# Up projections of two squared-ReLU layers as seven block products each (Strassen's scheme)

## The reference

```python
D_FF_2 = 4 * D_MODEL            # 4096
def sqrelu_mlp(h, w1, w2):
    a = jnp.square(jax.nn.relu(h @ w1))
    return a @ w2
...
h = h + sqrelu_mlp(rmsnorm_2(h, mlp_norm[i]), mlp_w1[i], mlp_w2[i])
```

## Time and profile before

| what | value |
| --- | --- |
| three executions | 2059.59, 2059.64 and 2062.62 us, median 2059.64 |
| profiled execution: span from first to last instruction | 2057.4 us |
| its instructions | 31378 |
| PE, weight loads (PEld), DVE, ACT, POOL busy | 1962.2, 1617.8, 1056.4, 742.9, 1060.0 us |
| DMA engines, mean busy share of the hardware queue | 31.8%, 80 GB/s read |

### The profile page before, as it was taken

One profiled execution on the slowest core, in us unless ns is written; L12 is line 12 of the kernel. 1 busy time (PEld: TensorE's weight loads), 2 busy tenths in 40 slices (PEclk: granted clock), 3 DMA queues, 4 the chain that ended last, 5 costly groups with the idle time before them and its releaser, 6 DMA issues.

```text
span 2057.4 us, 31378 instructions
## 1 busy us (share of the span) xinstructions
PE 1962.2 (95%) x10733; PEld 1617.8 (79%) x10733; DVE 1056.4 (51%) x1640; ACT 742.9 (36%) x1263; POOL 1060.0 (52%) x591
## 2 busy tenths in 40 slices
PE   8999989899999999889999999999998899999997
PEld 5679967778878787667778888887877788888886
DVE  6797846836687776796342313232137724222132
ACT  4335444533222224354432222233227642222223
POOL 5566747356747545662554444455445264444442
PEclk9999999999999999999999999999999999999999
DMA  4344013153333332101323333334346333333332
GB/s 138 78 112 117 23 42 98 31 113 92 95 89 102 92 92 78 36 2 33 100 84 102 92 102 92 92 94 108 94 109 156 84 100 101 92 102 92 97 94 86
DMA packets 345028, 181.87 MB, mean 88 GB/s; under 512 B 28527, under 2 KB 336103, under 8 KB 344935
## 3 DMA queue, kind: packets, MB, share of 16 engines
q1 hardware_dynamic: 343872, 179.91, 31.8%
q10 hardware_dynamic: 1062, 0.75, 0.1%
HBM read 162.73 MB, written 2.10 MB: 80 GB/s over the span
## 4 chain that ended last, share of the span: by engine, by line
PE 57%; issue 13%; POOL 9%; DVE 7%; POOLq 6%; ACT 3%; DVEq 2%; DMA 1%; SPq 1%; ACTq 0%
PE ACC L1625 16%; PE ACC L1631 16%; PE ACC L1626 16%; POOL WL L1254 7%; POOLq L1268 2%; POOLq L1479 1%; POOLq L1467 1%; PE ST L2097 1%; PE ACC L1797 1%; POOL GC L1478 1%; ACT WH L627 1%; POOL GT L1466 1%; SPq L586 1%; DVE DS L2281 1%; PE O L1754 0%
## 5 line engine op out<-in xcount | busy, mean ns | idle before, releaser
L1254 POOL TENSOR_TENSOR WL<-RAW,WH 128x1024 fp32r<-128x1024 f32 (+1 forms) x292 | 691.0, 2369 | 730.9 <-ACT WH L627 674.7
L1625 PE MATMUL ACC<-PH,WH 128*128 128x512 f32 x1248 | 493.6, 395 | 8.1 <-DVE PL L2206 2.8
L1626 PE MATMUL ACC<-PL,WH 128*128 128x512 f32 x1248 | 488.4, 391 | 0.0
L627 ACT ACTIVATE WH<-RAW 128x1024 fp32r<-128x1024 f32 (+1 forms) x292 | 301.0, 1032 | 450.3 <-PE ACC L1631 413.5
L1625 PE MATMUL ACC<-QH,WH 128*128 128x512 f32 (+1 forms) x1136 | 429.4, 382 | 12.7 <-ACT WH L627 6.9
L1626 PE MATMUL ACC<-QL,WH 128*128 128x512 f32 (+1 forms) x1136 | 425.7, 379 | 0.0
L1631 PE MATMUL ACC<-PH,WL 128*128 128x512 f32 x1248 | 312.8, 393 | 0.0
L1625 PEld LDWEIGHTS ACC<-PH,WH 128*128 128x128 f32 x1248 | 235.7, 189 | 66.3 <-DVE PL L2206 4.4
L1631 PE MATMUL ACC<-QH,WL 128*128 128x512 f32 (+1 forms) x1136 | 270.5, 379 | 6.5 <-POOL WL L1254 3.7
L1631 PEld LDWEIGHTS ACC<-PH,WL 128*128 128x128 f32 x1248 | 234.5, 188 | 52.7 <-issue 3.3
L1626 PEld LDWEIGHTS ACC<-PL,WH 128*128 128x128 f32 x1248 | 235.7, 189 | 48.8 <-issue 1.0
(11 more groups left out here) (448 smaller groups left out, 2548.3 us busy)
## 6 DMA issues: line engine op xcount, KB each, us to landing
RAW<-in_mlp_w_dram SPq DMA_DIRECT2D x128, 512.0 KB, 4.0
RAW<-in_w_gate_dram SPq DMA_DIRECT2D x22, 512.0 KB, 3.8
RAW<-in_w_up_dram SPq DMA_DIRECT2D x22, 512.0 KB, 3.8
RAW<-in_w_in_dram SPq DMA_DIRECT2D x16, 512.0 KB, 3.9
RAW<-in_w_down_dram SPq DMA_DIRECT2D x16, 512.0 KB, 4.1
RAW<-in_ssm_w_glu_dram SPq DMA_DIRECT2D x16, 512.0 KB, 3.8
RAW<-in_w_kvf_dram SPq DMA_DIRECT2D x16, 512.0 KB, 4.0
RAW<-in_w_out_dram SPq DMA_DIRECT2D x16, 256.0 KB, 2.8
```

The costliest lines, as they stand in the source:

```text
L627: act.activation(WH[:, s, 0:kc], RAW[:, s, 0:kc], ACT.Copy).then_inc(w_hi, 1)
L1254: pool.tensor_tensor(WL[:, s, 0:kc], RAW[:, s, 0:kc], WH[:, s, 0:kc], ALU.subtract).then_inc(w_lo, 1)
L1625: pe.matmul(ACC[s][:, 0:n], WH[:, s, k, :], xh[:, k, :], start=(k == 0), stop=False)
L1626: pe.matmul(ACC[s][:, 0:n], WH[:, s, k, :], xl[:, k, :], start=False, stop=False)
```

## The change

In each of the two layers, the eight up units of a group become two quads q. A quad is 512 hidden channels by 512 tokens by 1024 contracted channels, seen as a 2 x 2 block matrix product in Strassen's scheme (Winograd's form): the rows split into the even and the odd chunks of 128 channels, the columns into two pairs of 128, the tokens into two halves. Seven products (FAST = 7) take the place of eight blocks; a product is 24 matmuls of 256 columns.

Weights: SP loads the four blocks A11, A12, A21, A22 (two buffers of the last) of a quad, and DVE makes four sums of them: S1 = A21 + A22, S3 = A11 - A21, S2 = S1 - A11, and later S2 = A12 - S2. ACT rounds and POOL makes the remainder of each of the seven factors A11, S1, S2, A12, S3, S2, A22, into a ring of three slots. Operand: per pair of chunks DVE makes seven halves or differences of halves (TS, 128 x 256 each) where one scaled tile stood, ACT rounds them to FBH (two, then five of them) and DVE makes FBL. Results: banks FA and FE (two each) and FB; ACT copies three intermediate banks (PC1, PC5, PC6), DVE adds them to banks to make the blocks of HB, applies relu and RS, ACT squares and rounds, DVE makes the low part. The sums of the next quad, or of the next group during its last down units, are placed between these on DVE. The memsets of POOL move behind layer 0. The eight matmuls that keep PE busy at the start of either layer are gone.

```diff
+FAST = 7
-_MLP = [[(f"{_n}{_l}{_g}", 8) for _g in range(GROUPS) for _n in ("up", "dn")] for _l in range(2)]
+_MLP = [[(f"{_n}{_l}{_g}", {"up": 2 * FAST, "dn": 8}[_n]) for _g in range(GROUPS) for _n in ("up", "dn")] for _l in range(2)]
...
+RING = (2, 1, 0)
+OPERAND = (1, 0, 2, 5, 3, 6, 4)
...
+        def factor(n, j):
+            return (A11, S1, S2, A12, S3, S2, A22[n % 2])[j][:]
...
+            def round_factor(l, g, q, j):
+                n, u = quad_index(l, g, q), quad_unit(l, g, q) + j
+                if j in (0, 3, 6):
+                    k = {0: 0, 3: 1, 6: 3 + n % 2}[j]
+                    act.wait_ge(blk_in[k], BLK + 16 * ((n if j < 6 else n // 2) + 1))
+                else:
+                    act.wait_ge(s_made, 4 * n + {1: 1, 2: 3, 4: 2, 5: 4}[j])
+                act.wait_ge(unit_done, u - 1 if q == 0 and j == 1 else u - 2)
+                act.activation(high_weights(q, j), factor(n, j), ACT.Copy).then_inc(w_hi, 1)
...
+            def operand_high(l, i, b):
+                cols = slice(2, 7) if b else slice(0, 2)
+                act.wait_ge(ts_ready, TSR + KC * l + 2 * i + b + 1)
+                of = TS[:, 3:8, :] if b else TS[:, 0:2, :]
+                act.activation(FBH[l][:, bass.ds(i, 1), cols, :].rearrange("p o j t -> p (o j) t"), of, ACT.Copy).then_inc(op_hi, 1)
+                square(norm, 2 * i + b, X, b)
...
# ACT, in mlp(l), one group
+                    round_factor(l, g, 0, 1)
+                    for q in range(2):
+                        round_factor(l, g, q, 2)
+                        if q:
+                            block_squared(g, 0, 2)
+                        copied(l, g, q, 1)
+                        round_factor(l, g, q, 3)
+                        if q:
+                            block_high(g, 0, 2)
+                            block_squared(g, 0, 3)
+                        copied(l, g, q, 2)
...
+                        round_factor(l, g, q, 4)
+                        if q:
+                            block_high(g, 0, 3)
+                        copied(l, g, q, 3)
+                        round_factor(l, g, q, 5)
+                        round_factor(l, g, q, 6)
+                        block_squared(g, q, 0)
+                        if q == 0:
+                            round_factor(l, g, 1, 0)
...
+                        block_high(g, q, 0)
+                        block_squared(g, q, 1)
+                        if q == 0:
+                            round_factor(l, g, 1, 1)
+                        block_high(g, q, 1)
...
# POOL
+            def remainder_factor(l, g, q, j):
+                n, u = quad_index(l, g, q), quad_unit(l, g, q) + j
+                pool.wait_ge(w_hi, u + 1)
+                pool.tensor_tensor(low_weights(q, j), factor(n, j), high_weights(q, j), ALU.subtract).then_inc(w_lo, 1)
...
# PE
+            def product(l, g, q, j):
+                n, u = quad_index(l, g, q), quad_unit(l, g, q) + j
+                bank_ = (FA[n % 2], FE[n % 2], FA[n % 2], FB, FA[n % 2], FE[n % 2], FA[n % 2])[j]
+                begins = j in (0, 1, 3)
...
+                pe.wait_ge(w_hi, u + 1)
+                if j == 0 and n:
+                    pe.wait_ge(hid_ready, blocks_done(l, g, q) - (4 if n % (2 * GROUPS) else 0))
+                elif j == 2:
+                    pe.wait_ge(p_copied, PRD + 3 * n + 1)
+                elif j == 3 and n:
+                    pe.wait_ge(p_summed, PRD + 3 * n - 2)
+                elif j == 4:
+                    pe.wait_ge(p_copied, PRD + 3 * n + 3)
+                elif j == 6:
+                    pe.wait_ge(p_summed, PRD + 3 * n + 2)
...
+                pe.wait_ge(w_lo, u + 1)
...
+                    unit(START[f"dn{l}{g}"], 0, *h, chunks=(hid_lo, HIDDEN[f"mlp{l}"] + g * KC, (4, 4, 4, 4, 7, 7, 8, 8)))
...
# DVE, the sums (fourth_sum waits for the remainder of factor 2, second_sum for that of factor 5 of the quad before)
+            def second_sum(l, g, q):
+                n = quad_index(l, g, q)
+                if n:
+                    dve.wait_ge(w_lo, unit_of(n - 1) + 6)
+                dve.tensor_tensor(flat(S2), flat(S1), flat(A11), ALU.subtract).then_inc(s_made, 1)
...
+            def fourth_sum(l, g, q):
+                n = quad_index(l, g, q)
+                dve.wait_ge(blk_in[1], BLK + 16 * (n + 1))
+                dve.wait_ge(w_lo, quad_unit(l, g, q) + 3)
+                dve.tensor_tensor(flat(S2), flat(A12), flat(S2), ALU.subtract).then_inc(s_made, 1)
...
+                def block(g, q, e):
+                    n, u = quad_index(l, g, q), quad_unit(l, g, q)
+                    rows, cols = PART[e]
+                    h, rs = HB[:, rows, cols], RS[:, cols][:, None, :].to_broadcast([P, 2, T // 2])
+                    dve.wait_ge(unit_done, u + 4 + e)
+                    if e < 3:
+                        dve.wait_ge(p_copied, PRD + 3 * n + (1, 2, 3)[e])
+                        to, of = ((PC1, FB), (PC5, FA[n % 2]), (PC6, FE[n % 2]))[e]
+                        ins = dve.tensor_tensor(h, pairs_of(of), to[:], ALU.add).then_inc(p_summed, 1)
+                        dve.drain()
+                        dve.scalar_tensor_tensor(h, h, 0.0, rs, ALU.max, ALU.mult).then_inc(hid_ready, 1)
+                    else:
+                        dve.scalar_tensor_tensor(h, pairs_of(FA[n % 2]), 0.0, rs, ALU.max, ALU.mult).then_inc(hid_ready, 1)
...
# DVE, in mlp(l)
+                scales(norm, D)
                 for g in range(GROUPS):
+                    for q in range(2):
+                        fourth_sum(l, g, q)
+                        if q == 0:
+                            first_sum(l, g, 1)
+                        else:
+                            block_low(g, 0, 2)
+                            block_low(g, 0, 3)
+                        block(g, q, 0)
+                        block(g, q, 1)
+                        dve.sem_inc(unit_out, FAST)
+                        block_low(g, q, 0)
+                        if q == 0:
+                            third_sum(l, g, 1)
+                        block(g, q, 2)
+                        block_low(g, q, 1)
+                        if q == 0:
+                            second_sum(l, g, 1)
+                        block(g, q, 3)
+                    block_low(g, 1, 2)
+                    block_low(g, 1, 3)
                     if g < GROUPS - 1:
+                        for c in range(KC):
+                            down(g, c)
+                            if c == KC - 2:
+                                sums(l, g + 1, 0)
...
# DVE, ahead of layer 0 (in layer 1 attended_out in the place of glu)
+            with dve.Fori(0, 3) as i:
+                for b in range(2):
+                    glu(2 * i + b)
+                    operand(0, i, b)
+            glu(6)
+            operand(0, 3, 0)
+            sums(0, 0, 0)
+            glu(7)
+            operand(0, 3, 1)
```

More of the change, by code:

```diff
@@ L1119, in _, with glu @@
             act.wait_ge(hid_lo, HIDDEN["s5"] + KC)
-            with act.Fori(0, 4) as i:
+            def glu(i, last=False):
                 for b in range(2):
@@ new lines, in last_down @@
+                def last_down(i, last=False):
+                    for s in range(2):
+                        c = 2 * i + s
+                        if last and s:
+                            round_weights(START["kv"], 0, KC, SKIP["kv"])
+                        if not last:
+                            round_weights(START[name] + c + 2, s, KC, SKIP[name])
+                        prepare("kv", c, "kv_norm_2", PH[:, bass.ds(c, 1), :], s, (unit_out, START[name] + c + 1))
+                with act.Fori(0, 3) as i:
+                    last_down(i)
@@ L1155, in mlp1_end @@
+                last_down(3, True)
             def mlp1_end():
@@ L2144, in mlp @@
+            def mlp(l, h):
+                for g in range(GROUPS):
+                    for q in range(2):
+                        for j in range(FAST):
+                            product(l, g, q, j)
+                    unit(START[f"dn{l}{g}"], 0, *h, chunks=(hid_lo, HIDDEN[f"mlp{l}"] + g * KC, (4, 4, 4, 4, 7, 7, 8, 8)))
+                    unit(START[f"dn{l}{g}"] + 1, 1, *h)
                     if l == 0 or g < GROUPS - 1:
```

334 lines of the change are left out of this document (250 added, 84 removed).

## The result

The changed kernel takes **2156.29 us** (median; 2155.61 to 2160.35) where the kernel before took 2059.61 in the same comparison: a ratio of 1.0473, 95% interval 1.0458 to 1.0487. The forecast was 2132 with a range of 2083 to 2170 and slower at 0.88.

What follows compares the result with a forecast made beforehand. PE, busy 95%, was taken to bound the kernel before, and DVE and POOL alternating to bind after. Groups +53, starts +12, s5glu +6 and wo +1.5 gave +72.5 on the 2057.4 span: median 2132 us, range 2083 to 2170.

Steps and rivals of the forecast that it cites:

- PE's work: Up stretch: seven products of 2.88 us replace four units of 5.44, 1.60 us less per quad, 25.6 us for 16 quads.
- A group, +6.6: Each group of up and down units takes 6.6 us longer through DVE's late sums, blocks and lows; +53 us for eight.
- wait of 2.4 us ahead of product 13: Second quad of a group: PE waits from 41.5 for the addition of block 1, done at 43.9.
- The clock: Rival: PE's granted clock dips behind each of two waits per group, 1.7 us each; at most 2159 us; chance 0.14.
- DVE and POOL alternate: Up stretch: DVE operations with two SBUF inputs and POOL remainders exclude each other for a whole instruction, 11 against 7 per quad.
- the rival in which the port doesn't bind: Up stretch: DVE's turns fall into POOL's gaps and PE sets the pace, -3.0 us per group, 2055 us; chance 0.12.
- that in which only the sum of both counts: Rival: in the up stretch DVE wins ties or only both engines' sum counts, +3 us per group, 2103; chance 0.2.
- Starts, +12: Start of both layers: a longer chain on DVE and ACT delays factor 1, +6 us each, between +2 and +10 each.
- Gates and wo, +7.5 with bounds 0 and 12: s5glu and wo: longer operand preparation delays ACT's rounding of the next weights, +6 us in s5glu and +1.5 in wo.
- Between, nothing: Stretch between layer 0 and wo's stage: the forecast sum has no term for it.
- Moved memsets, nothing: The two memsets, 0.95 us each, moved from layer 0's start to before FWL: no cost; 1.9 us if uncovered.
- DMA at nothing: Factor loads: same bytes, landing in 4.0 us and asked for at least 10 us ahead, so no cost.

Runs made afterwards that it cites:

- a4: The changed kernel with 24 and 16 filler matmuls on PE in its waits for product 9 and in the first down unit; median 2153.07 us (1.0436).
- a1: The changed kernel with POOL's remainders of the up factors replaced by two memsets of the same tile; executed once, span 2066.7 us, period 84.7.
- b2: b1's order, second sum ahead of the third, and 13 of a group's 14 remainders moved from POOL to DVE; median 2077.61 us (1.0078).
- a3: The changed kernel with the second quad's second sum on DVE moved right behind the first quad's block 1; median 2138.97 us (1.0377).
- b1: The changed kernel with the next weights' rounding and remainder ahead of the operand's rounding and square in gates and wo; median 2148.41 us (1.0414).
- d1: c1 without its holding matmuls, first quad's sums and factor loads moved into the four units before each layer, wo's remainders on DVE; median 2058.46 us (0.9987).
- e1: d1 with the gate weights' remainder on DVE and the load of wo's fourth unit ahead of the factors; median 2048.52 us (0.9941).
- a2: The changed kernel with 2 instead of 8 third-pass matmuls in each product; executed once, span 2149.9 us, period 94.4.
- c1: b2 with layer-start sums and roundings reordered, wo's operand low parts one unit later, and 16 matmuls to hold PE's activity; median 2071.30 us (1.0046).

## Why the prediction was right, and where it was not

- **PE's work**: right. 2.88 us a product, by the third passes.
- **A group, +6.6**: mechanism and places right, size 7.7. Its schedule can be laid beside the trace, from 1166.0: first sum over at 12.9 (12.8 forecast), relu of block 0 at 15.7 (15.45), the second sum at 27.8 (27.9), product 9 started at 30.0 (29.0), addition of block 1 at 43.8 (43.9), last low part at 52.4 (53.1), first down unit over at 56.8 (55.9). Product 9 is 1.0 late although its rounding was over at 28.9: it also needs its bank, and the copy that frees it stands behind that rounding, which the prediction had in ACT's order but didn't count for product 9. What it lacked is the clock behind the second wait, 0.72 in the first down unit; filling the waits gave 1.4 a group (a4). The forecast wait of 2.4 us ahead of product 13 isn't seen in the kernel after, since the lower clock behind the first wait takes its place; a4 shows it, 2.18. The clock was a rival of its own with up to 1.7 us for each dip; it came together with the forecast case, one dip in the open and the other hidden by that wait.
- **DVE and POOL alternate**: shown, by a1 (period 84.7) and from the other side by b2 (85.1). The rival in which the port doesn't bind fell with the result; that in which only the sum of both counts (+3 a group) fell as well, at +7.7, and even a3 is at +4.7.
- **Starts, +12**: 11.6. The sum is right by luck, since 7.9 and 3.7 stand for 6 and 6. The wait is the one forecast: product 1 waits for factor 1 behind the last operand, in both layers. In layer 0 factor 1 is rounded 10.4 us behind the last unit's end and not 7.3, because DVE makes the second and third sum ahead of the gate's product, which the prediction left out there; and behind the wait product 1 runs at a clock of 0.50 (1070 to 1074), which it left out too. In layer 1 the same sums are counted in wo instead, ahead of its last addition.

```profile
1057.86 3.41 DVE L3267 TENSOR_TENSOR FS<-A,A 128x1024 f32<-128x1024 f32 x1
1061.36 1.23 DVE L3273 TENSOR_TENSOR FS<-FS,A 128x1024 f32<-128x1024 f32 x1
...
1070.15 0.58 PE L2357 MATMUL FOUR<-FBH,WH 128*128 128x256 f32 x1 [7.54 <-ACT WH L1045]
```

- **Gates and wo, +7.5 with bounds 0 and 12**: the step that failed; 23.8. In the gates the prediction had the right wait and the right length of the chain (2.5 us more; 2.6 in the trace), but took its slack of 0.8 us from c = 6, where no table load stands ahead of the rounding. Behind the odd gates one does, before as after, and the kernel before already lost 1.0 us there (11.87 for 10.88). So the chain counts in full, and the wait of 3 us brings a clock of 0.71 from 987 to 992: 3.8, 3.9 and 1.5 us for the three odd gates where the forecast had 1.7, and 0.3 to 0.5 for the even ones where it had 0.3. For wo it gave "some 0.4 for odd c", reading ACT's order alone. The measured 12.7 did not fall with ACT's order (b1, 55.2) but did when the remainders went to DVE (d1 and e1, 43.9 in the end): it is mostly the shared path, the prediction's own rule for a group, which it did not apply to the stage that got six more DVE operations per pair of units, the scaling among them.
- **Between, nothing**: +5.8 in this profile, of which 2.6 lies ahead of kv's column sums and 2.8 in the attention's last unit at a lower clock (0.67 from 1692.6 to 1702.5). The 2.6 begin with the load of kv's first weights, for which ACT waits in every kernel: its rounding starts with layer 0's last addition before, 1.1 us behind it in after, and PE's first matmuls then run at a lower clock. Over all ten changed kernels that rounding starts between 0.5 us ahead of the addition and 1.7 behind, and the stretch is +0.5 (a2) to +6.6 (b1) over before with the same operations. So this is mostly spread; a small cost of the change isn't excluded, since all lie above the one trace of before.
- **Moved memsets, nothing**: right. From kv's column sums to its first output are 6.7 us before and after.
- **DMA at nothing**: nearly right. A factor lands in 6.8 us instead of 4.0 (page, part 6), and DVE waited 1.7 us in all for one; a late load of wo's weights, moved behind factors, cost 3.3 in d1.

```profile
A<-in_mlp_w_dram SPq DMA_DIRECT2D x64, 512.0 KB, 6.8
```

One share in the prediction is off without effect: seven remainders of 2.40 in 20.16 us are 83% of POOL's time and leave 17%, not 84 and 15.

Still open: the share of the clock beyond the 1.4 us a group that a4 gave back, why the kv load lands earlier or later, and how much of b2's gain is its order.

## What to carry to other kernels

In this kernel the algorithm that trades matmuls for additions pays on DVE and POOL, and these two had to be added up nearly as one wherever both read SBUF: given to the one engine that does them faster, each remainder took 1.22 us instead of 2.40. Add up that path stage by stage, also in the stages that only prepare operands; where the sum passes PE's time, reordering gave little (3 of 7.7 us in a group, next to nothing in wo), and where it doesn't, it gave all (the gates). In an in-order engine, put what the next unit needs (a rounding, a copy that frees a bank) ahead of what waits for another engine.

## What the runs showed of the hardware that was not expected

- A DVE scaling of one tile by a column is held by a POOL subtraction like one with two tiles: 2.71 us against 0.49. A difference of 256 elements is held as well: 2.62 against 0.42 in after's wo.
- A POOL memset beside a DVE sum neither holds it nor is held: 0.95 us for 1024 elements, and 1.22 for the sum (a1).
- DVE alone with 34.2 us of work in 40 feeds PE without a gap (e1), where much the same work split between DVE and POOL left waits of 4.04 and 2.44 us in a group.
- Matmuls meant to hold the clock help only ahead of the wait that they fill; behind it they ran at the lower clock, 0.23 us each (c1, 16 in 3.62) instead of 0.13 (a4, 24 in 3.03).
